# Sixteen routed experts: the second block of 128 rows is turned in its own expert's branch

## The reference

```
for e in range(N_EXPERTS):                      # 16
    a, u = jnp.split(t @ w_ei[e], 2, axis=-1)   # 1024 -> 2 x 512
    y = y + gate[:, e:e + 1] * ((jax.nn.silu(a) * u) @ w_eo[e])   # 512 -> 1024
```

## Time and profile before

| | us |
|---|---|
| median of three runs | 1334.46 |
| lowest and highest | 1333.02, 1336.57 |
| time of the profiled execution | 1336.53 |
| its span in the trace | 1334.9 |
| PE busy | 1255.9 (94%) |
| experts on PE, first row transpose to last matmul | 868.5 to 1310.0 |
| a short expert with no wait on PE (e6) | 19.1 |
| a long expert (e5) | 35.5 |

### The profile page before, as it was taken

One profiled execution on the slowest core, in us unless ns is written; L12 is line 12 of the kernel. 1 busy time (PEld: TensorE's weight loads), 2 busy tenths in 40 slices (PEclk: granted clock), 3 DMA queues, 4 the chain that ended last, 5 costly groups with the idle time before them and its releaser, 6 DMA issues.

```text
span 1334.9 us, 19105 instructions
## 1 busy us (share of the span) xinstructions
PE 1255.9 (94%) x7182; PEld 1032.6 (77%) x7183; DVE 702.0 (53%) x890; ACT 622.2 (47%) x844; POOL 352.0 (26%) x306
## 2 busy tenths in 40 slices
PE   5999999999999999999999999589999999989992
PEld 4888866788878888966788878467788888868871
DVE  4233367422476333267522365867854765785456
ACT  4222367532233322366632230757744665775445
POOL 0532000000120332000000030157643756575333
PEclk9999999999999999999999999689999999999997
DMA  6742100023363322200022544479977978898653
GB/s 220 249 155 95 64 1 1 32 95 122 130 231 116 126 95 95 96 1 1 1 96 84 186 153 177 131 265 293 342 252 217 299 241 299 264 341 280 179 182 154
DMA packets 63522, 212.33 MB, mean 159 GB/s; under 512 B 12391, under 2 KB 12903, under 8 KB 62648
## 3 DMA queue, kind: packets, MB, share of 16 engines
q1 hardware_dynamic: 49052, 178.24, 38.7%
q0 software_dynamic: 11808, 24.59, 7.1%
q10 hardware_dynamic: 2592, 8.53, 1.6%
HBM read 199.00 MB, written 34.25 MB: 175 GB/s over the span
## 4 chain that ended last, share of the span: by engine, by line
PE 84%; DVE 5%; ACT 3%; DMA 3%; issue 2%; POOL 2%; SPq 0%; POOLq 0%; DVEq 0%; ACTq 0%
PE banks L737 23%; PE banks L738 22%; PE banks L739 22%; PE banks L846 3%; PE banks L882 2%; PE banks L917 2%; PE banks L1037 2%; PE banks L924 2%; DMA x_rows<-x_rows,slot_tab 1%; PE banks L857 1%; PE banks L771 1%; DMA moe_raw<-in_expert_w 1%; POOL gated L607 1%; DVE moe_lo L1476 1%; ACT moe_hi L1324 1%
## 5 line engine op out<-in xcount | busy, mean ns | idle before, releaser
L1495 DVE TENSOR_TENSOR wlo<-raw,whi 128x2048 fp32r<-128x2048 f32 (+1 forms) x52 | 116.0, 2231 | 176.6 <-ACT whi L1153 176.6
L1476 DVE TENSOR_TENSOR moe_lo<-moe_raw,moe_hi 128x2048 fp32r<-128x2048 f32 x81 | 183.6, 2287 | 32.2 <-ACT moe_hi L1324 31.6
L1324 ACT ACTIVATE moe_hi<-moe_raw 128x2048 fp32r<-128x2048 f32 x96 | 182.9, 1916 | 30.9 <-PE banks L739 17.1
L737 PE MATMUL banks<-xT,whi 128*128 128x512 f32 x448 | 176.0, 393 | 0.0
L738 PE MATMUL banks<-xT,whi 128*128 128x512 f32 x448 | 175.5, 392 | 0.0
L739 PE MATMUL banks<-xT,wlo 128*128 128x512 f32 x448 | 175.4, 391 | 0.0
L607 POOL TENSOR_TENSOR gated<-gated,kqv 128x512 f32<-128x512 f32 x16 | 25.3, 1596 | 489.9 <-DVE kqv L1640 489.9
L737 PE MATMUL banks<-moe_lo,xeh 128*128 128x512 f32 x368 | 146.7, 399 | 5.9 <-DVE moe_lo L1476 4.2
L737 PE MATMUL banks<-wlo,xT 128*128 128x256 f32 (+1 forms) x448 | 136.0, 304 | 13.2 <-DVE wlo L1495 13.2
L738 PE MATMUL banks<-moe_hi,xeh 128*128 128x512 f32 x368 | 144.7, 393 | 0.0
L739 PE MATMUL banks<-moe_hi,xel 128*128 128x512 f32 x368 | 144.7, 393 | 0.0
(11 more groups left out here) (273 smaller groups left out, 2324.2 us busy)
## 6 DMA issues: line engine op xcount, KB each, us to landing
moe_raw<-in_expert_w SPq DMA_DIRECT2D x192, 512.0 KB, 5.9
raw<-in_front_w SPq DMA_DIRECT2D x104, 512.0 KB, 4.9
toeplitz_rows<-bias_rows POOLq DMA_DIRECT2D x4, 1152.0 KB, 13.5
kqv<-in_x_turned SPq DMA_DIRECT2D x8, 512.0 KB, 7.6
pt<-in_x SPq DMA_DIRECT2D x2, 2048.0 KB, 10.2
x_rows<-pt ACTq DMA_DIRECT2D x8, 512.0 KB, 2.7
token_sums<-pt ACTq DMA_DIRECT2D x8, 512.0 KB, 3.7
moe_raw<-token_sums SPq DMA_DIRECT2D x8, 512.0 KB, 8.0
```

The lines of the kernel that those rows point to most:

```text
L737: mm(dst, left[0], right[1], start=first, stop=False)
L1324: A(moe_hi[m % SPLIT_E], moe_raw[m % RAW_E], ACT.Copy).then_inc(e_hi, 1)
L1476: V.tensor_tensor(moe_lo[m % SPLIT_E], moe_raw[m % RAW_E], moe_hi[m % SPLIT_E].bitcast(F32), ALU.subtract).then_inc(lo_sem(m % ECH), 1)
L1495: V.tensor_tensor(view(lo, shape), view(raw[c % 2], shape), view(hi, shape).bitcast(F32), ALU.subtract).then_inc(w_split, 1)
```

## The change

The rows of an expert are now turned by blocks instead of both blocks at once. A group is four pieces of one block. The next expert's block one is turned in two groups, at the places where groups 2 and 3 stood. Nothing stands behind `turn_acts(0)` any more. Block two of an expert is turned at the beginning of that expert's own long branch, into banks 1 and 3; the short branch doesn't turn it, and signals instead with its first matmul. ACT and DVE have no branch: they do both groups of block two for every expert, at a new place, behind the two copies to `y_sb` and ahead of `e_split` of chunk 5'. In a long expert chunks 0 and 1 are multiplied for block one, and then for block two, once `xe_lo` says that block two's groups are done. The gathers signal for each block apart, and the first expert's turning waits for block one alone.

```
-            def turn_rows(b, z, gathers, groups, banks=(2, 3, 2, 3)):
-                pe.wait_ge(rows_in[b], gathers * 32)
-                for g in groups:
...
-            turn_rows(0, 0, 1, range(4), FIRST_BANKS)
+            def turn_rows(b, c, g):
+                tb = bank[ROW_BANKS[c][g]]
+                for q in range(4):
+                    k = 4 * g + q
+                    last = nc.tensor.transpose(tb[:, q * P:(q + 1) * P], x_rows[b][:, c * D + k * P:c * D + (k + 1) * P], ident)
+                last.then_inc(rows_T, 1)
+            pe.wait_ge(rows0_in[0], 16)
+            for g in range(2):
+                turn_rows(0, 0, g)
             def step(pair, b, width, more=True):
                 z = pair * 2 + b
-                pe.wait_ge(xe_lo, z * 4 + 4 + 2)
+                if width > P:
+                    pe.wait_ge(rows1_in[b], pair * 16 + 16)
+                    turn_rows(b, 1, 0)
+                    pe.wait_ge(xe_lo, z * 4 + 2 + 2)
+                    turn_rows(b, 1, 1)
...
+                pe.wait_ge(h_done, z * HALVES + 1)
+                for c in range(2):
+                    pe.wait_ge(lo_sem(c), lo_by(z, c))
+                    pe.wait_ge(xe_lo, z * 4 + 2 + c + 1)
+                    last = in_part(c, 0)
+                    if width == P:
+                        last.then_inc(e_used, 1)
+                if width > P:
+                    for c in range(2):
+                        pe.wait_ge(xe_lo, z * 4 + 2 + 4)
+                        in_part(c, 1).then_inc(e_used, 1)
...
                     if c == 2:
                         turn_acts(0)
-                        rows_of_next(0, 1)
...
                 out_part(0, 0, (0,))
-                rows_of_next(2)
+                row_of_next(0)
                 turn_acts(1)
                 last = out_part(0, 0, (1,))
...
-                rows_of_next(3)
+                row_of_next(1)
...
             def expert(pair, b):                      # on DVE; ACT likewise
...
                 acts_lo(z, 0)
-                rows_lo(1 - b, z + 1, (0, 1))
                 gated_half(z, 1)
-                rows_lo(1 - b, z + 1, (2,))
+                row_lo(1 - b, z + 1, 0, 0)
                 acts_lo(z, 1)
-                rows_lo(1 - b, z + 1, (3,))
+                row_lo(1 - b, z + 1, 0, 1)
                 e_split(pair, b * ECH + 3 + SPLIT_E)
                 e_split(pair, b * ECH + 4 + SPLIT_E)
...
                 for d in range(2):
                     V.tensor_scalar(y_sb[b][:, D + d * 512:D + (d + 1) * 512], bank[6 + d][:, :], slot_gate(b, 1), None,
                                     ALU.mult).then_inc(y_dve, 1)
+                for g in range(2):
+                    row_lo(1 - b, z + 1, 1, g)
                 e_split(pair, b * ECH + XCH + 1 + SPLIT_E)
```

More of the change, by code:

```diff
@@ L424, in encoder_kernel @@
         y_gone = sem("y_gone")
-        rows_in = [sem(f"rows_in{i}") for i in range(2)]
+        rows0_in = [sem(f"rows0_in{i}") for i in range(2)]
+        rows1_in = [sem(f"rows1_in{i}") for i in range(2)]
         rows_T, xe_hi, xe_lo = sem("rows_T"), sem("xe_hi"), sem("xe_lo")
@@ L1062, in turn_acts, with row_of_next @@
                     last.then_inc(h_turned, 1)
[L1064 removed]
+                def row_of_next(g):
                     if more:
[L1066 to L1073 removed]
+                        pe.wait_ge(rows0_in[1 - b], pair * 16 + (16 if b == 0 else 32))
+                        if g == 1:
+                            pe.wait_ge(xe_lo, z * 4 + 2 + 4)
+                        turn_rows(1 - b, 0, g)
@@ new lines, in in_part @@
+                def in_part(c, r):
+                    n, half, kh = b * ECH + c, c // 2, c % 2
+                    w = [t[n % SPLIT_E].rearrange("p (k n) -> p k n", k=KD // 2) for t in (moe_hi, moe_lo)]
+                    for k in range(KD // 2):
+                        last = mm3(bank[2 - 2 * half + r][:, :], [v[:, kh * (KD // 2) + k, r * P:(r + 1) * P] for v in xv],
+                                   [v[:, k] for v in w], kh == 0 and k == 0, kh == 1 and k == KD // 2 - 1)
+                        if width == P and c == 0 and k == 0:
+                            last.then_inc(rows_T, 2)
+                    return last
@@ L1074, in step @@
+                pe.wait_ge(h_done, z * HALVES + 2)
+                for c in range(2, XCH):
+                    pe.wait_ge(lo_sem(c), lo_by(z, c))
                     for r in range(width // P):
-                        for k in range(KD // 2):
-                            last = mm3(bank[2 - 2 * half + r][:, :], [v[:, kh * (KD // 2) + k, r * P:(r + 1) * P] for v in xv],
-                                       [v[:, k] for v in w], kh == 0 and k == 0, kh == 1 and k == KD // 2 - 1)
+                        last = in_part(c, r)
@@ L1338, in _, with row_hi @@
             act.wait_ge(logit_ready, NT + 2)
[L1340 to L1343, removed]
+            def row_hi(b, z, c, g):
+                if (c, g) == (1, 1):
+                    act.wait_ge(xe_lo, z * 4 + 2 + 2)
+                act.wait_ge(rows_T, z * 4 + 2 * c + g + 1 + 8)
+                A(row_part(xe[b][0], c, g), turned_part(c, g), ACT.Copy).then_inc(xe_hi, 1)
             for c in range(EARLY_E, RAW_E + 1):
@@ L1364, in _ @@
                 e_split(0, c)
-            rows_hi(0, 0, range(4), FIRST_BANKS)
+            for c in range(2):
+                for g in range(2):
+                    row_hi(0, 0, c, g)
             act.wait_ge(counted, 1)
@@ L1368, in gated_half @@
             def gated_half(z, half):
+                if half == 0:
+                    act.wait_ge(xe_lo, z * 4 + 2 + 4)
                 act.wait_ge(e_used, SPLIT_E + z * ECH + 2 * half + 2)
@@ L1395, in expert @@
                     A(y_sb[b][:, d * 512:(d + 1) * 512], bank[4 + d][:, :], ACT.Copy, scale=slot_gate(b, 0)).then_inc(y_act, 1)
+                for g in range(2):
+                    row_hi(1 - b, z + 1, 1, g)
                 e_split(pair, b * ECH + XCH + 1 + SPLIT_E)
```

49 lines of the change are left out of this document (25 added, 24 removed).

## The result

The changed kernel takes 1344.04 us (median of five runs, 1341.2 to 1350.08), the kernel before 1336.04 in the same comparison. The ratio is 1.0068 [1.0052, 1.0084]: 0.7% slower. The slowdown is thus 0.4 to 0.7%, and a variant whose ratio lies between these two is not told apart from the changed kernel.

The account below looks back on a forecast made before the run. Short experts were bound by DVE's chain to hT plus 7.0 us, long ones by PE. Terms 1.2 + 1.4 + 4.3 + 0.2 - 0.9 = +6.2 us gave 1342.7 on the profiled execution, 1340.7 on the median; range 1332 to 1346.

Parts of the forecast that it names:

- What the profile would show: Listed hT waits in nearly all short experts, xel waits about 1 us in four long ones, first matmul at 871.
- Transposes removed: Every step loses eight transposes (0.79 us): no gain in short experts, paid back at the beginning of long ones; 0.
- Copies, short behind long: In three short experts behind long ones, row copies at the chain's beginning delay the second product 0.4 us each: +1.2.
- The long step's wait: In four long experts behind short ones, PE waits for block two's copies: 0.5 + 1.3 + 1.35 + 1.1 = +4.3 us.
- Short behind short: In e3, e11, e12, copies lengthen DVE's chain or partly fill waits for weights: 0.2, 1.2 and 0, sum +1.4 us.
- rival of the fallen clock: Granted clock falls behind PE's longer waits, each costing 1.6 us; with three, +11, 1345.5 us; chance 0.12.
- The last expert: In e15, transposes at the beginning (0.8 us) aren't paid back, but PE waits 1.05 for busy DVE: +0.2.
- The start: Ahead of e0, first matmul 2.5 us earlier, less 1.6 charged for a low clock after idle time: -0.9.
- PE as the bound: Rival: 72 fewer transposes win 7.1 us, with 2.5 at the start 9.6: 1325 us; chance 0.09.
- No change: Rival: long steps' waits are covered and the start gives its whole 2.5: +0.3, 1335 us; chance 0.18.
- code-loading rival: Changed branch lengths remove or add a gap like those ahead of e1 and e2: 1337 or 1344.5 us; chance 0.07.

Follow-up runs that it names:

- second series: The changed kernel, unedited, timed once more in seven runs against the kernel before: ratio 1.0044, 1342.3 us.
- e6: Not a run: a short expert of the kernel, behind a long one; 19.1 us long before, 19.4 in the changed kernel.
- e4, e13: Not a run: a long expert of the kernel, behind a short one; 35.51 us before, 35.95 in the changed kernel.
- the kernel with fewer of them: Kernel before with 6 of each step's 16 row transposes left out, all copies kept: ratio 0.9967, 1331.8 us.
- small copies: Changed kernel with block two's copies cut to two columns of each piece, PE multiplying block one instead of block two: ratio 1.0018, 1339.1 us.
- e5, e14: Not a run: a long expert of the kernel, behind a long one; 35.51 us both before and in the changed kernel.
- e7: Not a run: a long expert of the kernel, behind a short one; 35.50 us before, 36.09 in the changed kernel.
- second profile: Profile of one execution of the unedited changed kernel, from its repeat timing in seven runs: this execution takes 1345.95 us.
- e11: Not a run: a short expert of the kernel, behind a short one; 20.54 us before, 22.82 in the changed kernel.
- e3: Not a run: a short expert of the kernel, behind a short one; e1, e2 and e3 together 65.49 us before, 65.83 in the changed kernel.
- e12: Not a run: a short expert of the kernel, behind a short one; 22.20 us before, 21.87 in the changed kernel.
- e0: Not a run: the first expert of the kernel, a short one; 21.84 us before, 24.52 in the changed kernel.
- the earlier gather: Changed kernel without POOL's wait between the gathers of the first and second experts' rows: ratio 1.0083.
- e1: Not a run: the second expert of the kernel, a short one, behind a gap; 23.42 us in the changed kernel's first profile.
- e2: Not a run: the third expert of the kernel, a short one, behind a gap; 20.90 us in the changed kernel's first profile.
- the subtraction first: Changed kernel with DVE's hT subtraction of half 0 moved ahead of the split of chunk 1': ratio 1.0046, 1341.65 us.
- the copies ahead of y_sb: Changed kernel with block two's copies directly ahead of the y_sb copies, without and with the hT subtraction ahead of chunk 1': ratio 1.0084 each.
- small copies and the subtraction first: Changed kernel with block two's copies cut to two columns and the hT subtraction ahead of the split of chunk 1': ratio 1.0002.
- filled time ahead of it: Changed kernel with sixteen unused identity transposes in PE's idle time ahead of the first expert: ratio 1.0062.
- the fill: Changed kernel with four unused matmuls in PE's idle time ahead of short experts' second product: ratio 1.0044, 1341.57 us.
- e10: Not a run: a short expert of the kernel, behind a long one; 19.15 us in the kernel with fewer of them.
- e15: Not a run: the last expert of the kernel, a long one; 35.98 us before, 36.79 in the changed kernel.

## Why the prediction was right, and where its sizes were off

The direction and the mechanism were right. The time agrees on the profiled execution (1342.29, forecast 1342.7) partly by luck, since the terms were off in both directions and it was one of the faster executions. On the median, where 1340.7 was forecast, the measured 1344.04 is 3.3 more; 1.6 of that is that before's own median rose from 1334.46 to 1336.04 with two more runs. Where a change of 6.2 was forecast, the medians of this series differ by 8.0, and the second series by 0.44%, or 5.9. What the profile would show came in part: the listed waits for hT, e6 at 19.4 and the first matmul at 870.5 did, but the waits for xel were a quarter of the 1 us forecast, and none is listed in e4 and e13.

*Transposes removed: 0.* Right, shown by the kernel with fewer of them (short 19.13, long 0.7 less each), by the 0.80 of waiting with small copies, and, for the transposes paid back at a long step's beginning, by e5 and e14 at 35.51 in before and after.

*Copies, short behind long: +1.2.* Measured +0.9, 0.3 each, and taken away by the small copies.

*The long step's wait: +4.3.* It is there, and goes with the small copies, but measured +2.1 (0.4, 0.6, 0.6 and 0.4). The forecast took the time of y_sb behind PE's start from before (6.1 in e7). DVE and ACT of after:

```profile
1055.83 1.41 DVE L1940 TENSOR_SCALAR y_sb<-banks,slot_ids 128x512 f32<-128x512 f32 x2
1057.15 1.28 DVE L1899 TENSOR_TENSOR xel<-banks,xeh 128x512 fp32r<-128x512 f32 x2
```

```profile
1051.67 1.92 ACT L1355 ACTIVATE moe_hi<-moe_raw 128x2048 fp32r<-128x2048 f32 x1 [0.41 <-DMA moe_raw<-in_expert_w]
```

The same row of ACT in before:

```profile
1051.64 1.92 ACT L1324 ACTIVATE moe_hi<-moe_raw 128x2048 fp32r<-128x2048 f32 x1 [1.09 <-DMA moe_raw<-in_expert_w]
```

With e7 starting at 1051.73, y_sb is done 5.4 behind the start. Its time on DVE hangs on the split of chunk 4', which ACT begins when the chunk is there: 0.65 behind the start of e7 in before, at the start in after. Of these 0.7, 0.3 are e6's own new length, and 0.4 that the chunk comes sooner behind the start of e6 (19.4 for 19.8; the second profile has 19.4 too). The lengthened short step pays for part of the long one's wait. That step, carrying over a distance from PE's start for work that is paced by a transfer, is the one that was most off in size.

*Short behind short: +1.4, of it e11 1.2.* e11's chain, DVE and PE of after:

```profile
1169.32 2.28 DVE L1513 TENSOR_TENSOR moe_lo<-moe_raw,moe_hi 128x2048 fp32r<-128x2048 f32 x1
1171.52 0.68 DVE L1915 TENSOR_TENSOR h_full<-silu,banks 128x512 f32<-128x512 f32 x1
```

```profile
1162.84 0.40 PE L749 MATMUL banks<-moe_lo,xeh 128*128 128x512 f32 x1
...
1177.36 0.47 PE L749 MATMUL banks<-moe_lo,hT 128*128 128x512 f32 x1 [1.90 <-DVE hT L1921]
...
1178.50 0.63 PE L750 MATMUL banks<-moe_hi,hT 128*128 128x512 f32 x1
```

From start to second product 14.52, before 13.48: +1.04. The other 1.24 of its 2.3 are behind the product, where the granted clock fell (matmuls of 0.63). That is the rival of the fallen clock, in one place of three. It was not there in the second profile, where e11 is 21.55. The +1.04 is the copies in DVE's unbroken work, but with small copies the weights held e11 as long, so 1.0 would not have been saved by making them cheap. e3 and e12 gave 0.0 and -0.3 for 0.2 and 0: right to take little there; in the second profile, with the clock fallen in e12, it is +0.7 there.

*The last expert: +0.2.* Measured +0.8: its waits of 1.05 and 0.51 stayed (now 1.08 and 0.43). The forecast read the 1.05 as a busy DVE with a time of its own. But the DVE work ahead of it, the last layer norm, and the transposes both follow earlier steps of the same expert, and they all moved with PE (the hT subtraction by 0.79). The small copies don't take these 0.8 away either: the same two waits are there, 0.43 and 1.05.

*The start: -0.9.* Measured -0.4. PE, DVE and ACT of after at e0:

```profile
864.63 1.09 PE L1045 MATMUL banks<-ident,x_rows 128*128 128x128 f32 x8 [1.19 <-DMA x_rows<-x_rows,slot_tab]
870.48 0.80 PE L749 MATMUL banks<-moe_lo,xeh 128*128 128x512 f32 x1 [4.75 <-DVE xel L1899]
871.07 0.63 PE L750 MATMUL banks<-moe_hi,xeh 128*128 128x512 f32 x1
```

```profile
879.85 0.69 DVE L1915 TENSOR_TENSOR h_full<-silu,banks 128x512 f32<-128x512 f32 x1 [5.77 <-DMA x_rows<-x_rows,slot_tab]
```

```profile
878.09 0.60 ACT L1406 ACTIVATE silu<-banks 128x512 f32<-128x512 f32 x1 [0.73 <-PE banks L751]
```

The first matmul is 3.0 earlier, not 2.5, at the low clock, as charged: the 36 matmuls start over 10.1 us (870.48 to 880.61) where 8.18 is usual, 1.9 more for the 1.6 charged. In before the clock was 0.50 too while the sixteen transposes ran (868.5 to 871.4), and full again before the first matmul. The step that lacks is the gated half. It starts 1.76 behind the silu where 0.63 is usual, because it waits for the gather: 1.1 more. With the earlier gather it starts 0.64 behind the silu (879.87, 879.23), so the 1.1 is the gather's. The second product of e0 comes at 885.69, only 0.35 earlier than before's 886.04 (873.52 + 12.52). The Trainium skill (TensorE: Matmul & The Clock Gate, Part 1), whose rule of sustained activity spoke against this start, agrees with the trace: the clock was 0.50 from 870.4 to 874.2 behind the wait of 4.75.

*The rivals.* PE as the bound falls with e6 at 19.44 and not 18.3. No change falls with the ratio. The gaps ahead of e1 and e2, which the code-loading rival was about, are still there. Their sum moved by 0.3 us in the first profile, so little of its 5.8 is theirs; in the second it moved by 2.5, of 9.4 in all. What share they have in the medians is not known, and no run tried code loading by itself.

**Open.** What sets the length of the gaps ahead of e1 and e2 (1.4 to 4.6 us over all profiles) was not tried by itself. Of what paces chunk 4' the traces settle one half. It began on ACT 19.4 to 20.2 us behind the start of e6 in before, after and the two with the subtraction first whose copies stand behind y_sb, and 22.4 and 21.6 with the copies ahead of y_sb, where DVE's splits and with them the free buffers come later. SyncE issues its load 0.2 us behind the end of DVE's split of chunk 0', which frees the buffer. In after:

```profile
1041.91 1.00 SPq L541 DMA_DIRECT2D moe_raw<-in_expert_w  x2
```

That is 9.6 behind the start of e6 (1032.29). It is 9.3 in before and with small copies and the subtraction first, 9.6 with the subtraction first alone, and 10.3 in the two with the copies ahead of y_sb. So the buffer accounts for 0.7 to 1.0 of the 2 to 3 us of delay in those two, and for at most 0.3 in the others. The rest, 9.8 to 12.1 us from issue to ACT's start, is the load itself, together with the chunks around it. What makes it longer was not tried.

## What to carry to other kernels

A wait too short to be listed can be the bound: compare the start of the consumer with the end of its producer, and if the distance is the same in every repetition (0.15 us here), the producer sets the time, and work taken from the consumer buys idle time. When two or three engines and a transfer are nearly balanced, as in these short experts, work moved from the end of a chain to its beginning costs what the idle time there doesn't absorb (0.3 us of 1.2 in e6, 1.0 in e11), and time won in one step can come back as a wait for the transfer in the next. For such a wait ask what paces it, and measure from that, not from the waiting engine.

## What the runs showed of the hardware

- A listed wait is less than what it costs. In e7 of after PE's row says 0.27, yet the expert is 0.59 longer: a matmul shows 0.39 us at a pitch of 0.23, so the first 0.16 of a delay is not idle time, and the first matmul behind the wait takes 0.34 to the next one in place of 0.23 (0.54 in all):

```profile
1058.49 0.50 PE L749 MATMUL banks<-moe_lo,xeh 128*128 128x512 f32 x1 [0.27 <-DVE xel L1899]
1058.83 0.39 PE L750 MATMUL banks<-moe_hi,xeh 128*128 128x512 f32 x1
```

- The granted clock can fall when PE is busy again, behind the gap: 1.3 us behind one of 3.04 with filled time ahead of it (872.04), and 0.8 us behind one of 1.90 in e11. The same gap of 1.90 in e3 (1.91) and in the second profile of e11 had no such fall, while one of 1.90 in e12 of that profile had it.
- At the beginning of a short expert the low clock costs nearly its whole: in e1 and e2 of after, behind the gaps, the second product starts 13.76 and 13.86 us behind the start, and 12.26 and 12.25 with the fill, where the clock was full. The chain to it begins with PE's matmuls.
- The two gaps ahead of e1 and e2 vary between executions of one kernel: 2.10 and 2.47 us in the first profile of after, 2.27 and 4.47 in the second.
